# Gate tables copied after 70 row products instead of 76, one-hots of each half ahead of the GELU wait, and 14 instead of 16 row sums behind the first residual

## The chip, the cores and the metric

One core of a Trainium2 chip runs the whole program. The metric is device time in microseconds (us), the median over runs of the same program; smaller is better.

## What is computed

The program computes two transformer blocks over 256 tokens of width 1024, in float32. What matters here is the feed-forward part of the first block, which looks up single-neuron experts (8 heads, 16 experts of each head for every token, out of 16384):

```
def per_chunk(args):
    xc, ec, gc = args
    u = expert_u[ec]
    a = jnp.einsum('cd,chkd->chk', xc, u).astype(jnp.float32)
    w = (jax.nn.gelu(a) * gc).astype(xc.dtype)
    return jnp.einsum('chk,chkd->cd', w, expert_v[ec])
```

`ec` are the chosen experts of a token, `gc` their gates (a softmax over the chosen scores). The result is added to the residual stream, and the second block begins with matrix products on that sum.

## The kernel before

**Two ways to the same sum.** The 152 first tokens (DENSE) are computed densely: all 16384 experts, in 128 blocks of 128. An up block (L902, TensorE) is eight matmuls (16 records in the trace) into one PSUM bank; ScalarE takes its GELU (L1412) into the table `H`; VectorE multiplies `H` by the gates, which are zero for experts that a token didn't choose; a down block (L910) multiplies by the second weight table. The last 104 tokens are computed sparsely: for each of 107 pairs of columns a row of `u_rows` is fetched for each of 128 partitions (an indirect DMA issued by GpSimd, L2488, 128 rows of 4096 bytes), VectorE multiplies it by the token and adds up (L1901, a **row product**), the 107 results go through GELU and are weighed with their gates, and 107 fetched rows of `v_rows` are added up with these weights (L2022, a **row sum**; the first of each part is L2018).

**The fetches.** All 214 fetches go through seven buffers in one fixed order: products 0 to 95, sums 0 to 63, products 96 to 106, sums 64 to 106. GpSimd issues a fetch as soon as VectorE is through with the row seven places earlier. The two are called turns here: turn n is the n-th of these 214, and `row_turns(upto)` runs them until `upto` are done.

**The stream.** Weights come through a ring of four slots of 1 MB, loaded from the SyncE queue (L457). A slot holds two expert blocks and is loaded again when TensorE has used both.

**Order on TensorE.** The first 64 up blocks run with nothing between them. The gates and indices of the tokens (`routed`) are transposed ahead of the last eight of these (L942). Then TensorE waits for `sel_ready` (two copies of the transposed gate tables out of PSUM into `sel16`, VectorE, L2039) and goes into `mixed(0)`: up blocks 64 to 127, with `gates(0)` to `gates(18)` between them. Each is 16 small matmuls (L923) on one-hot tables of eight tokens, which VectorE writes in `one_hots` (L2055, L2056, L2058); they spread the gates over the experts of a half. `gates(0)` stands behind one block, `gates(1)` behind four more, and then three or four blocks lie between two of them. `gates(q)` waits for the one-hots q and for `apply_gates` q-2. `mixed(1)` is the same with down blocks 0 to 63 and `gates(19)` to `gates(37)` for the second half of the experts; 64 more down blocks follow.

**Order on VectorE.** 64 turns lie between the routing steps. `row_dots(DOTS_FIRST - dots_done[0])` brings them to 76, then come the two copies, and then the loop over the halves `hf` and the 19 groups `g`: the one-hots of g, `apply_gates` of g-1 (L2065, multiplies `H` in place, waits for TensorE's gates), and turns up to `a + (b - a) * (g + 1) // 19`, with (a, b) = (76, 116) in the first half and (116, 164) in the second. At the head of each half it waits until ScalarE's GELU has written that half of `H` (`expert_gelu`). Behind the loop come the remaining turns but the last 16 sums, the residual of the first 128 tokens (four times L2094, which TensorE's last down block releases), and the last 16 sums. TensorE meanwhile computes the first layer of the second block for tokens 0 to 127 (up to L1016), waits for all 107 sums, folds them in (L1029), and VectorE adds the residual of tokens 128 to 255.

Of the kernel before, what the change touches and what calls it, by code (L numbers as in the profile page):

```python
# [37 lines left out]
HALF_BLOCKS = EXPERT_BLOCKS // 2  # L38
# [14 lines left out]
DOTS_GATES = DOTS_EARLY + sum(DOTS_SCORES)  # L53
DOTS_SUMS = (4, 4, 4, 4, 3)
DOTS_PICK = 3
DOTS_FIRST = 76
TURNS_UP = 116
TURNS_DOWN = 164
GATES_AT = 22
WEIGH_AT = 8  # L60
WEIGH_GROUP = 7
LAST_ADDS = 16
ROWS = 7
U_FIRST = 96

# [90 lines left out]
class Count:  # L156
# [10 lines left out]
    def link(self, ins):  # L167

        self.inc(ins)
        self.eng.wait_ge(self.sem, self.n + self.more)  # L170


def build(nc, streams, small_d, first_d, second_d, mem_d, x_d, u_rows, v_rows, held_d, kv_scratch, out_d):
    ctx = ExitStack()
    with ctx:
# [3 lines left out]
        def sem(name):  # L179
            return ctx.enter_context(nc.semaphore(name))  # L180
# [214 lines left out]
        expert_psum, expert_gelu = sem("expert_psum"), sem("expert_gelu")  # L395
# [1192 lines left out]
        def _(dve):  # L1588
# [243 lines left out]
            for q in range(2):  # L1832
                dve.wait_ge(slot_done, START["merge"] + 2 * q + 2)
                for j in range(4):
                    n = 4 * q + j
                    tmp = merge_tmp.rearrange("p (b t) -> p b t", b=2)
                    g = gT.rearrange("p (b j) t -> p b j t", b=2)[:, :, n, :]
# [57 lines left out]
            def row_dots(count):  # L1895

                for m in range(dots_done[0], dots_done[0] + count):
                    f = u_fetch(m)
                    b = f % ROWS
                    dve.wait_ge(row_in[b], 16 * (f // ROWS + 1))  # L1900
                    dve.tensor_tensor_reduce(fetched[:, b, :], fetched[:, b, :], x_sparse[:, m // PAIRS_HALF, :], 1.0, 0.0, ALU.mult, ALU.add,  # L1901
                                             dots[:, 0, m:m + 1]).then_inc(dot_ready, 1)
                dots_done[0] += count
# [106 lines left out]
            def row_adds(count):  # L2010

                for m in range(adds_done[0], adds_done[0] + count):
                    f, part = v_fetch(m), m // PAIRS_HALF
                    b = f % ROWS
                    dve.wait_ge(row_in[b], 16 * (f // ROWS + 1))
                    total = sparse_sum[:, part, :]
                    if m % PAIRS_HALF == 0:
                        dve.tensor_scalar(total, fetched[:, b, :], dots[:, 0, m:m + 1], None, ALU.mult)\  # L2018
                            .then_inc(row_added, 1)
                    else:  # L2020
                        dve.wait_ge(row_added, m)
                        dve.scalar_tensor_tensor(total, fetched[:, b, :], dots[:, 0, m:m + 1], total,  # L2022
                                                 ALU.mult, ALU.add).then_inc(row_added, 1)
                adds_done[0] += count

            def row_turns(upto):

                for turn in range(dots_done[0] + adds_done[0], upto):
                    if turn < U_FIRST or U_FIRST + PAIRS_HALF <= turn < CHUNKS + PAIRS_HALF:
                        row_dots(1)  # L2030
                    else:
                        row_adds(1)

            row_dots(DOTS_FIRST - dots_done[0])

# [8 lines left out]
            def one_hots(g, q, b, hf, first=False):  # L2044

                if not first:
                    dve.wait_ge(gates_psum, q - 1)

                def key(j, n):
                    return sel16[:, j, g * GROUP:(g + 1) * GROUP].unsqueeze(2).to_broadcast([P, GROUP, n])  # L2050

                def numbers(a, n):
                    return iota16[:, a:a + n].unsqueeze(1).to_broadcast([P, GROUP, n])

                dve.tensor_tensor(e2[:, b], numbers(0, P), key(1, P), ALU.is_equal)  # L2055
                link(dve.tensor_tensor(e_same[:, b], numbers(hf * HEAD, HEAD), key(0, HEAD), ALU.is_equal))  # L2056
                gates_of = sel16[:, 2:4, g * GROUP:(g + 1) * GROUP].unsqueeze(3).to_broadcast([P, 2, GROUP, HEAD])
                dve.tensor_tensor(e1[:, b], e_same[:, b].unsqueeze(1).to_broadcast([P, 2, GROUP, HEAD]), gates_of,  # L2058
                                  ALU.mult).then_inc(e_ready, 1)

            def apply_gates(g, q, b, hf):

                dve.wait_ge(gates_psum, q + 1)
                h = H[:, hf * HALF_BLOCKS:(hf + 1) * HALF_BLOCKS, g * GROUP:(g + 1) * GROUP]
                dve.scalar_tensor_tensor(h, h, 1.0 / GSCALE, ps[:, 2 + b, :].rearrange("p (t n) -> p n t", t=GROUP),  # L2065
                                         ALU.mult, ALU.mult).then_inc(gates_applied, 1)

            def weigh(c, gelu, ready):

                dve.wait_ge(gelu, 1)  # L2070
                dve.tensor_tensor(dots[:, 0, c], dots[:, 1, c], pairs[:, 1, c], ALU.mult).then_inc(ready, 1)
                dve.wait_ge(ready, 1)

            for hf in range(2):
                dve.wait_ge(expert_gelu, HALF_BLOCKS * (hf + 1))
                for g in range(GROUPS):
                    if hf == 0 and g == WEIGH_GROUP:
                        dve.wait_ge(pairs_in, 16 * (3 + SETS_B))
                        weigh(slice(0, PAIRS_HALF), dot_gelu, weight_ready)
                    q = hf * GROUPS + g  # L2080
                    one_hots(g, q, q % 2, hf, first=(hf == 0 and g < 2))
                    if g:
                        apply_gates(g - 1, q - 1, (q - 1) % 2, hf)
                    a, b = ((DOTS_FIRST, TURNS_UP), (TURNS_UP, TURNS_DOWN))[hf]
                    row_turns(a + (b - a) * (g + 1) // GROUPS)
                apply_gates(GROUPS - 1, (hf + 1) * GROUPS - 1, ((hf + 1) * GROUPS - 1) % 2, hf)
            row_adds(PAIRS_HALF - adds_done[0])
            row_dots(CHUNKS - dots_done[0])
            weigh(slice(PAIRS_HALF, CHUNKS), dot_gelu_b, weight_b_ready)
            row_adds(CHUNKS - LAST_ADDS - adds_done[0])  # L2090

# [626 lines left out]
```

## Time and profile before

| | |
|---|---|
| median of 3 runs | 1790.42 us (1789.12 to 1792.3) |
| the profiled execution: time, span | 1789.55 us, 1787.8 us |
| granted TensorE clock, mean over the span | 0.992 |
| TensorE matmuls busy | 98% of the span |
| VectorE busy | 63% |
| ScalarE, GpSimd busy | 13%, 17% |

The profiled execution's time is 1.75 us more than its span. It lies 0.87 us below the median of the three runs. Times in the rows below are us from the span's start.

### The profile page before, as it was taken

The page shows a single profiled execution, that of the slowest core. Times are in us where ns is not written, and L with a number is a line of the kernel's source. Part 1 is how long each engine was busy: PE and PEld are TensorE (multiplying, and loading weights), DVE is VectorE, ACT ScalarE, POOL GpSimd, SP SyncE. Part 2 cuts the span into 40 slices and gives each one's busy share as a digit, 9 for nine tenths or more (in the row PEclk, how much of TensorE's full clock was granted, in tenths as well). Part 3 has the DMA queues.
Part 4 walks back from the last instruction along what each step waited for, and adds up shares of the span by engine and source line. Part 5 has one row for each costly group of instructions (what it writes and reads, how often), then busy time and mean ns, then how long its engine had stood idle before and what let it go on. Part 6 is the DMA issues. An engine that isn't in the chain of part 4 may idle for free.

```text
span 1787.8 us, 29568 instructions
## 1 busy us (share of the span) xinstructions
PE 1745.0 (98%) x11801; PEld 1491.0 (83%) x11801; DVE 1119.7 (63%) x2415; ACT 240.6 (13%) x599; POOL 296.9 (17%) x282
## 2 busy tenths in 40 slices
PE   8999999999999899999999999999999999999996
PEld 7888566986999899999999867799965988699942
DVE  4742432798666888799533453269974763379964
ACT  1014520111414111000000011111100001111100
POOL 0010000144333343344422200000000000000000
PEclk9999999999999899999999999999999999999998
DMA  7535234499999999999999953365444535354551
GB/s 273 189 118 165 71 118 142 158 332 374 414 417 416 376 381 390 346 415 415 415 417 417 350 223 118 121 250 172 166 165 165 169 138 171 123 178 166 168 179 54
DMA packets 76609, 439.62 MB, mean 246 GB/s; under 512 B 8578, under 2 KB 8656, under 8 KB 37840
## 3 DMA queue, kind: packets, MB, share of 16 engines
q1 hardware_dynamic: 42624, 305.15, 45.9%
q0 software_dynamic: 32592, 125.92, 18.2%
q10 hardware_dynamic: 1280, 6.95, 1.0%
q8 instruction: 82, 1.34, 0.3%
q14 instruction: 31, 0.25, 0.0%
HBM read 432.67 MB, written 5.24 MB: 245 GB/s over the span
## 4 chain that ended last, share of the span: by engine, by line
PE 80%; DVE 9%; DMA 9%; issue 1%; ACT 1%; POOL 0%; SPq 0%; DVEq 0%; POOLq 0%
PE ps L1128 16%; PE ps L910 14%; PE ps L529 10%; PE ps L902 8%; DMA arena<-u_rows,sparse_pairs 7%; PE ps L573 7%; PE ps L1166 4%; PE ps L612 3%; PE ps L487 3%; DVE arena L1901 2%; PE ps L765 2%; PE ps L812 2%; PE ps L778 1%; DVE arena L2022 1%; PE ps L923 1%
## 5 line engine op out<-in xcount | busy, mean ns | idle before, releaser
L902 PE MATMUL ps<-xT,ring 128*128 128x152 f32 x2048 | 271.9, 295 | 9.4 <-DVE sel L2039 9.4
L902 PEld LDWEIGHTS ps<-xT,ring 128*128 128x128 f32 x2048 | 267.6, 191 | 9.7 <-DVE sel L2039 9.6
L910 PE MATMUL ps<-arena,ring 128*128 128x152 f32 (+1 forms) x2048 | 269.6, 293 | 0.5 <-DMA ring<-stream 0.5
L910 PEld LDWEIGHTS ps<-arena,ring 128*128 128x128 f32 x2048 | 265.5, 190 | 1.2 <-issue 1.2
L529 PE MATMUL ps<-ring,arena 128*128 128x512 f32 x416 | 181.4, 592 | 0.4 <-ACT arena L1476 0.4
L2022 DVE SCALAR_TENSOR_TENSOR arena<-arena,sparse_dots 128x1024 f32<-128x1024 f32 x105 | 134.7, 1283 | 66.8 <-DMA arena<-v_rows,sparse_pairs 61.5
L1901 DVE CUSTOM_DVE_ANT_0 arena<-arena 128x1024 f32<-128x1024 f32 x107 | 128.1, 1223 | 71.1 <-DMA arena<-u_rows,sparse_pairs 70.6
L2488 POOL DMA_INDIRECT arena<-v_rows,sparse_pairs x107 | 132.7, 1241 | 233.3 <-DVE arena L2022 184.7
L2488 POOL DMA_INDIRECT arena<-u_rows,sparse_pairs x107 | 127.3, 1190 | 178.3 <-DVE sparse_dots L1901 154.4
L2451 POOL TENSOR_SCALAR stat<-stat 128x1 f32<-128x1 f32 (+2 forms) x23 | 4.4, 191 | 916.5 <-DVE stat L2192 705.1
L529 PEld LDWEIGHTS ps<-ring,arena 128*128 128x128 f32 x416 | 78.0, 190 | 93.0 <-issue 92.3
L573 PEld LDWEIGHTS ps<-xT,ring 128*128 128x128 f32 x1344 | 152.2, 192 | 3.0 <-issue 2.9
L573 PE MATMUL ps<-xT,ring 128*128 128x128 f32 x1344 | 153.2, 275 | 0.0
L1128 PE MATMUL ps<-arena 128*128 128x128 f32 x1128 | 133.6, 275 | 0.0
L1128 PEld LDWEIGHTS ps<-arena 128*128 128x128 f32 x1128 | 129.7, 192 | 0.0
L1128 PE MATMUL ps<-xT,ring 128*128 128x128 f32 x752 | 91.7, 275 | 0.0
L1128 PEld LDWEIGHTS ps<-xT,ring 128*128 128x128 f32 x752 | 87.7, 192 | 0.0
L487 PE MATMUL ps<-xT,ring 128*128 128x256 f32 x288 | 65.9, 391 | 0.0
L487 PEld LDWEIGHTS ps<-xT,ring 128*128 128x128 f32 x288 | 56.3, 197 | 8.0
L1412 ACT ACTIVATE arena<-ps 128x152 f32 x128 | 38.0, 297 | 181.5 <-PE ps L902 181.3
L1750 DVE CUSTOM_DVE_ANT_0 arena<-ps,small 128x128 f32<-128x128 f32 (+1 forms) x48 | 14.6, 354 | 76.1 <-PE ps L700 48.0
L1166 PE MATMUL ps<-arena 128*128 128x512 f32 x112 | 52.8, 594 | 0.3
(341 smaller groups left out, 2244.0 us busy)
## 6 DMA issues: line engine op xcount, KB each, us to landing
ring<-stream SPq DMA_DIRECT2D x288, 1024.0 KB, 7.4
arena<-second_params POOLq DMA_DIRECT2D x6, 1024.0 KB, 5.5
arena<-kv_scratch POOLq DMA_DIRECT2D x2, 2048.0 KB, 14.3
kv_scratch<-arena ACTq DMA_DIRECT2D x2, 1024.0 KB, 11.0
arena<-held_params ACTq DMA_DIRECT2D x1, 2048.0 KB, 16.6
arena<-u_rows,sparse_pairs POOLq DMA_INDIRECT x107, 14.3
arena<-v_rows,sparse_pairs POOLq DMA_INDIRECT x107, 14.4
arena<-second_params POOLq DMA_DIRECT2D x1, 1536.0 KB, 6.6
```

The source lines that it names most:

```text
L487: ins = pe.matmul(ps[:, bank, t * T:(t + 1) * T], w[:, k * 2 * P + t * P:k * 2 * P + (t + 1) * P], act[:, k, :], start=(k == 0), stop=(k = ...
L529: ins = pe.matmul(ps[:, bank0 + 2 * o + hf, :], act_of(2 * s + k, i), held[s][:, k * D + hf * 512:k * D + (hf + 1) * 512], start=(bank0 + ...
L573: ins = pe.matmul(ps[:, bank, t * T + i * P:t * T + (i + 1) * P], held[s][:, k * 2 * P + t * P:k * 2 * P + (t + 1) * P], xT[:, k, i * P:(i ...
L612: ins = pe.matmul(ps[:, b0 + b, half * T:(half + 1) * T], x[:, k, :], weight[:, k, :], start=(k == 0), stop=(k == 3))
L902: ins = pe.matmul(ps[:, o % 2, 0:DENSE], w[:, (o % 2) * D + k * P:(o % 2) * D + (k + 1) * P], xT[:, k, 0:DENSE], start=(k == 0), stop=(k = ...
L910: ins = pe.matmul(ps[:, 4 + k // 2, c:c + DENSE], w[:, (o % 2) * D + k * P:(o % 2) * D + (k + 1) * P], H[:, n, :], start=False, stop=last, ...
L1128: ins = pe.matmul(ps[:, bank + b, c * P:(c + 1) * P], weight[:, k, :], x[:, k, :], start=(k == 0), stop=(k == 3))
L1166: return pe.matmul(ps[:, bank, :], x, weight, start=(m == 0), stop=(m == FT_PAIRS - 1 and bank < 4))
L1412: act.activation(H[:, n, :], ps[:, b, 0:DENSE], ACT.Gelu_apprx_tanh).then_inc(expert_gelu, 1)
L1901: dve.tensor_tensor_reduce(fetched[:, b, :], fetched[:, b, :], x_sparse[:, m // PAIRS_HALF, :], 1.0, 0.0, ALU.mult, ALU.add, dots[:, 0, m: ...
L2022: dve.scalar_tensor_tensor(total, fetched[:, b, :], dots[:, 0, m:m + 1], total, ALU.mult, ALU.add).then_inc(row_added, 1)
L2488: pool.indirect_dma_start(fetched[:, b, :], None, table, bass.IndirectOffsetOnAxis(ap=pairs[:, 0, m:m + 1].bitcast(U32), axis=0), bounds_c ...
```

## The change

Three edits, all in VectorE's order:

1. The copies of the gate tables stand behind 70 turns instead of 76. The loop of the first half then starts at a = 74 (`DOTS_TURN`), so its first group runs turns up to 76 (six of them, where it ran two up to 78), and the later groups reach b = 116 as before.
2. The wait for `expert_gelu` moves from the head of a half to behind the one-hots of group 1, ahead of the first `apply_gates` of the half. The one-hots of groups 0 and 1, and the turns of group 0, no longer stand behind it, in both halves.
3. `LAST_ADDS` is 14 instead of 16: two row sums move from behind the first residual to ahead of it.

```diff
-DOTS_FIRST = 76
+DOTS_FIRST = 70
+DOTS_TURN = 74
...
-LAST_ADDS = 16
+LAST_ADDS = 14
...
             for hf in range(2):
-                dve.wait_ge(expert_gelu, HALF_BLOCKS * (hf + 1))
                 for g in range(GROUPS):
                     if hf == 0 and g == WEIGH_GROUP:
                         dve.wait_ge(pairs_in, 16 * (3 + SETS_B))
                         weigh(slice(0, PAIRS_HALF), dot_gelu, weight_ready)
                     q = hf * GROUPS + g
                     one_hots(g, q, q % 2, hf, first=(hf == 0 and g < 2))
+                    if g == 1:
+                        dve.wait_ge(expert_gelu, HALF_BLOCKS * (hf + 1))
                     if g:
                         apply_gates(g - 1, q - 1, (q - 1) % 2, hf)
-                    a, b = ((DOTS_FIRST, TURNS_UP), (TURNS_UP, TURNS_DOWN))[hf]
+                    a, b = ((DOTS_TURN, TURNS_UP), (TURNS_UP, TURNS_DOWN))[hf]
                     row_turns(a + (b - a) * (g + 1) // GROUPS)
```

## Rows read from the trace of the kernel before

**Rows 1.** The page, busy time, share of the span and instructions of each engine.
```profile
PE 1745.0 (98%) x11801; PEld 1491.0 (83%) x11801; DVE 1119.7 (63%) x2415; ACT 240.6 (13%) x599; POOL 296.9 (17%) x282
```
**Rows 2.** The page's groups: count, busy us, mean ns, idle before and its releaser.
```profile
L902 PE MATMUL ps<-xT,ring 128*128 128x152 f32 x2048 | 271.9, 295 | 9.4 <-DVE sel L2039 9.4
...
L910 PE MATMUL ps<-arena,ring 128*128 128x152 f32 (+1 forms) x2048 | 269.6, 293 | 0.5 <-DMA ring<-stream 0.5
```
**Rows 3.** Timeline of TensorE: start, duration, instruction, count, idle before.
```profile
559.66 1.04 PE L942 MATMUL ps<-small,arena 128*128 128x128 f32 x8
560.53 16.78 PE L902 MATMUL ps<-xT,ring 128*128 128x152 f32 x128
586.72 4.22 PE L902 MATMUL ps<-xT,ring 128*128 128x152 f32 x16 [9.40 <-DVE sel L2039]
590.78 0.63 PE L923 MATMUL ps<-e 128*128 128x64 f16 x16
591.24 8.51 PE L902 MATMUL ps<-xT,ring 128*128 128x152 f32 x64
599.59 0.63 PE L923 MATMUL ps<-e 128*128 128x64 f16 x16
...
722.60 0.63 PE L923 MATMUL ps<-e 128*128 128x64 f16 x16
```
**Rows 4.** Windows: length, then PE, PEld, DVE, ACT, POOL busy; clock; DMA share; GB/s.
```profile
577.40:580.40 3.00, 0.00 (x0) 0.00 (x0) 1.23 (x2) 0.30 (x1) 1.17 (x2) 0.99 0.99 408
...
586.70:590.70 4.00, 3.98 (x16) 3.98 (x17) 3.97 (x4) 0.00 (x0) 0.99 (x1) 0.51 1.03 409
```
**Rows 5.** Timeline of VectorE around the two copies, in the same columns.
```profile
566.75 1.23 DVE L1901 CUSTOM_DVE_ANT_0 arena<-arena 128x1024 f32<-128x1024 f32 x1 [1.90 <-DMA arena<-u_rows,sparse_pairs]
...
584.66 1.23 DVE L1901 CUSTOM_DVE_ANT_0 arena<-arena 128x1024 f32<-128x1024 f32 x1 [2.17 <-DMA arena<-u_rows,sparse_pairs]
...
585.81 0.85 DVE L2039 CAST sel<-ps 128x96 f16<-128x96 f32 x2
586.70 1.25 DVE L2055 TENSOR_TENSOR e<-iota,sel 128x1024 f16<-128x1024 f16 x1
587.87 0.68 DVE L2056 TENSOR_TENSOR e_same<-iota,sel 128x512 f16<-128x512 f16 x1
588.58 1.23 DVE L2058 TENSOR_TENSOR e<-e_same,sel 128x1024 f16<-128x1024 f16 x1
```
**Rows 6.** DMA queues in 545 to 580 us: stream (q1), row fetches (q0), MB moved.
```profile
q1 hardware_dynamic: 1186, 8.67, 59.9%
q0 software_dynamic: 1616, 5.86, 41.7%
```
**Rows 7.** The same in 740 to 865 us, inside the second mixed stage.
```profile
q1 hardware_dynamic: 3950, 28.82, 56.2%
q0 software_dynamic: 6070, 22.11, 44.3%
```
**Rows 8.** Both queues in 945 to 985 us.
```profile
q1 hardware_dynamic: 1515, 11.08, 66.9%
q0 software_dynamic: 1537, 5.61, 34.7%
```
**Rows 9.** Timeline of VectorE and TensorE where the second half begins.
```profile
732.04 1.23 DVE L2055 TENSOR_TENSOR e<-iota,sel 128x1024 f16<-128x1024 f16 x1 [8.09 <-ACT arena L1412]
...
736.91 0.28 PE L923 MATMUL ps<-e 128*128 128x64 f16 x4
```
**Rows 10.** Timeline of VectorE: the first residual and the last sums.
```profile
1010.80 1.42 DVE L2094 TENSOR_TENSOR xT<-ps,arena 128x256 f32<-128x256 f32 x4 [22.03 <-PE ps L910]
1012.14 22.11 DVE L2022 SCALAR_TENSOR_TENSOR arena<-arena,sparse_dots 128x1024 f32<-128x1024 f32 x16
```
**Rows 11.** Timeline of TensorE at the same place.
```profile
1025.46 7.03 PE L1016 MATMUL ps<-arena,xT 128*128 128x512 f32 x16
1034.30 3.77 PE L1029 MATMUL ps<-small,arena 128*128 128x64 f32 x32 [1.81 <-DVE arena L2022]
```

## The prediction

> **What bounds the kernel now.** I read the page first: TensorE's matmuls are busy for 98% of the span [rows 1], so a change on VectorE can only pay where TensorE waits for VectorE, or where it makes TensorE wait. The page's groups name the first such place: the up blocks stand idle for 9.4 us, all of it in front of the gate tables' copies, while the down blocks lose 0.5 us, to the stream [rows 2]. The timeline shows it as one stall: the last block ahead of the mixed stage ends at 560.53 + 16.78 = 577.31, the next begins at 586.72 [rows 3]. VectorE spends that time on row products that wait for their DMA; the copies come at 585.81, at once behind the twelfth of them [rows 5]. Their input has been there since the transposes of 559.66 [rows 3], so only VectorE's order holds them back. The second place is the end of the lookup: TensorE ends L1016 at 1032.49 and waits 1.81 us for the last sum [rows 11].
>
> **Edit 1, the copies after 70 turns.** The twelve products behind the routing steps become six. The sixth starts at 566.75 and ends 1.15 later (584.66 to 585.81 is one) [rows 5]; the copies take 0.85 and end at 568.8. That is 8.5 us before TensorE asks for them at 577.31. The stall of 9.40 us goes whole.
>
> **The clock behind the stall.** The granted clock is still 0.99 in the first 3 us of the idle time, and 0.51 while the first block after it runs [rows 4], that is 1.2 GHz and not 2.4. That block takes from 586.72 to 590.78, 4.06 us; four blocks at full clock take 591.24 to 599.59, 2.09 each [rows 3]. Without the stall nothing lowers the clock here, so 4.06 - 2.09 = 1.97 us come on top. The bounds are 0 (the clock falls all the same, in a short wait that takes the stall's place) and 1.97; I take 1.97, since TensorE was busy without a break up to 577.31.
>
> **What is late next.** The six moved products now stand between the one-hots 0 and 1. One-hots 0 start at 568.8 and take 588.58 + 1.15 - 586.70 = 3.03 [rows 5], so they are ready at 571.8, and `gates(0)`, behind one block at 579.4, doesn't wait. Then come turns 70 to 75 (counted from 0). Their rows land as before, because each fetch is released by the product seven places earlier and those for 70 to 75 are all released by products that don't move. The last of them is waited for at 584.66 [rows 5]. It ends at 585.81; one-hots 1 are ready 3.03 later, at 588.84. TensorE reaches `gates(1)` without a wait at 577.31 + 2.09 + 0.46 + 8.35 = 588.21 (block 64, the gates' 590.78 to 591.24, four blocks) [rows 3]. So a wait of 0.63 us takes the stall's place. Bounds: 0 if that row lands 0.6 us earlier, 3.8 if it lands one row's time later; at 3.8 the clock could fall again, and 2.0 more go. I take 0.63: up to 577 the two kernels ask the DMA for the same, and of what comes after, only the stream's reloads differ.
> `gates(1)` stood at 599.59 and comes to 588.84: 9.40 + 1.97 - 0.63 = 10.75 us (the last digit by rounding).
>
> **The rows afterwards.** In the stall the stream paused and the row fetches caught up; that rest is now gone, so I check whether VectorE can follow. A row fetch is 128 x 4096 B = 0.524 MB. Ahead of the mixed stage the row queue moves 5.86 MB in 35 us, 167 GB/s, a row every 3.13 us, beside a stream of 8.67 MB, 248 GB/s [rows 6]. In the second mixed stage, where gates stand between the blocks and the stream asks for less, it is 22.11 MB in 125 us, 177 GB/s, a row every 2.96 us, beside 231 GB/s of stream [rows 7]. What is needed: one-hots 18 stand behind turn 112, which is 37 rows behind the one of 584.66. With a row every p us, `gates(18)` can't come before 584.66 + 37p + 1.4 (a sum: 22.11 / 16) + 3.03. Without waits it comes 722.60 - 599.59 = 123.0 us after `gates(1)` [rows 3], at 711.9. The rows set the end only from p = (711.9 - 589.1) / 37 = 3.32. At 2.96 to 3.13 they cost nothing. The bound from the other side is the row queue of 945 to 985: 5.61 MB in 40 us, 140 GB/s, p = 3.74 [rows 8]. I take 2.96 to 3.13 because the stage differs from that of rows 7 only in up for down blocks.
> The GpSimd queue gets its releases for turns 77 and on up to 3.9 us later than in the kernel before (0.85 of copies and 3.03 of one-hots stand ahead of turn 70 now); the fetches are queued seven deep, and that is inside p. The stream's queue only follows TensorE.
> The wait for the GELU of the first half, now behind one-hots 1, is empty: ScalarE is through with block 63 soon after 577.31, VectorE comes there at 588.8.
>
> **Edit 2, second half.** VectorE waits 8.09 us for the GELU at 732.04 [rows 9]; it will fill this with one-hots 19, two sums and one-hots 20. TensorE gains nothing: `gates(19)` runs at 736.91, its one-hots were ready at 732.04 + 3.03 = 735.1 [rows 9]. Cost and gain are 0; VectorE's head start, 8 us at most, only helps to cover late rows. If that cover were gone, it would show as waits of `gates` in the second mixed stage. No instruction is added, and the fetches released earlier reach a queue in which the stream has its lead.
>
> **Edit 3, 14 sums.** Sixteen sums of 1.38 us end at 1034.25 [rows 10]; fourteen end 2.76 earlier, at 1031.5, before TensorE's own end of L1016 at 1032.49 [rows 11]. The wait of 1.81 goes whole, bounds 0 and 1.81. The two moved sums, and the release of their fetches, stand in VectorE's idle time of 22.03 us ahead of the first residual [rows 10]. With TensorE 10.75 us earlier, and two more sums at 3.74 us of a row, 22.03 - 10.75 - 7.5 = 3.8 us of it remain even if the rows don't come a microsecond sooner. What follows (residual of the second tokens, parameter load, normalization) hangs on L1029 and moves with it.
>
> **Sum.** 10.75 + 1.81 = 12.6 us. Against the profiled execution: 1789.55 - 12.6 = 1777.0. It was 0.87 below the median, so against the median 1790.42 - 12.6 = 1777.8.
>
> **Rivals.**
> A. *Rows a little too slow.* From p = 3.32 each 0.1 us costs 3.7: at 3.4 three us go, at 3.5 6.7, which leaves a gain of 5.9. Or the row for turn 75 lands one row's time late: 3.1 and the clock's 2.0 go, 7.5 remain. For it: nearly all of the DMA's time is taken, and rows of 3.74 exist. Against it: rows 6 and 7. It gives 1780.5 to 1785.
> B. *The other sign: rows at 3.74 through the first mixed stage.* Mechanism: the stream's queue is never empty, takes its full share, and VectorE's one-hots wait for rows group after group. `gates(18)` then comes at 584.66 + 37 x 3.74 + 4.4 = 727.4, 4.8 us later than before, less the 1.8 of edit 3: 3.0 slower, 1793.4. It decides from p = (722.6 + 1.8 - 589.1) / 37 = 3.66. For it: rows 8. Against it: there the stream took 277 GB/s of 417, more than TensorE's pace asks of it, as after a delay; in 545 to 580 it kept TensorE busy with 248 [rows 6, 8].
> The Trainium skill's page "DMA: Bandwidth & Descriptors", section "SWDGE vs HWDGE vs iDMA", says that a DMA engine takes its queues in turn. With rows in packets of 4096 B and the stream in packets of 8192 B, that rule would leave the rows a third of some 412 GB/s, an estimate of 3.8 us a row, and by it the sum would come out as rival B. The trace shows that third in 945 to 985; in 545 to 580 the rows had 167 of 415 GB/s.
> C. *Given back:* the sums come late before the first residual, and TensorE, which can't start the next block without it, gives the 10.75 back there. The slack of 3.8 us would have to be overrun by as much, three rows' time at 3.74. Only edit 3 stays: 1790.42 - 1.8 = 1788.6.
>
> **How the numbers follow.** Forecast 0.76, A 0.14, B 0.06, C 0.04. The forecast's own range is 1776 to 1780: at the low end no wait at `gates(1)` (0.6) and the scatter of the runs, some 1.5; at the high end 1.5 of small waits in front of gates and the scatter. For eight in ten I reach upward into A: 1775.5 to 1783.5. About 0.2% (3.6 us) is what a measurement of this kernel can tell from no change. Faster by more than that: forecast and A, 0.90; within: C, 0.04; slower: B, 0.06.
>
> **What would show it.** Copies (L2039) at 568; no idle time of TensorE named after them; the clock at 1.00 from 560 to 600; a wait of some 0.6 us in front of the second `gates`, then none; VectorE waiting for u rows in the first groups, where it didn't before; no wait for the last sums at L1029 (at about 1021), VectorE's idle time ahead of the first residual 4 to 15 us instead of 22. The prediction is wrong if TensorE stands in front of several `gates` of the first mixed stage, or if the clock falls again near 580 to 590.

## The result, and the profile after

The changed kernel takes 1774.93 us (median of 4 runs, 1774.62 to 1775.13), the kernel before 1789.77 in the runs beside it (1787.53 to 1792.3): ratio 0.991, 95% interval 0.9894 to 0.9927. That is 14.8 us faster, where the forecast was 12.6, and 0.6 us below the range of the forecast. The changed kernel's four runs lie within 0.5 us, those of the kernel before within 4.8. Two of the 66 runs of the kernel before in the experiments below took 2113 and 4723 us and are left out of every comparison.

The page's groups of the changed kernel, as [rows 2] (count, busy us, mean ns, idle before). Line numbers are one or two higher than before:

```profile
L911 PE MATMUL ps<-arena,ring 128*128 128x152 f32 (+1 forms) x2048 | 269.7, 293 | 0.4 <-DMA ring<-stream 0.4
L903 PE MATMUL ps<-xT,ring 128*128 128x152 f32 x2048 | 269.8, 293 | 0.0
```

The 9.4 us of idle time of the up blocks are gone, and they are busy 2.1 us less (269.8 for 271.9): the block at half clock. The timeline of TensorE at the place of [rows 3]:

```profile
558.00 1.04 PE L943 MATMUL ps<-small,arena 128*128 128x128 f32 x8
558.87 18.88 PE L903 MATMUL ps<-xT,ring 128*128 128x152 f32 x144
577.59 0.63 PE L924 MATMUL ps<-e 128*128 128x64 f16 x16
578.05 8.51 PE L903 MATMUL ps<-xT,ring 128*128 128x152 f32 x64
586.83 0.64 PE L924 MATMUL ps<-e 128*128 128x64 f16 x16 [0.26 <-DVE e L2059]
...
709.84 0.63 PE L924 MATMUL ps<-e 128*128 128x64 f16 x16
```

The block ahead of the copies and the one behind them are one piece now (144 records). `gates(1)` waits 0.26 us, and no later gates wait: from there to `gates(18)` it is 123.0 us, as before [rows 3]. Two windows (length, TensorE busy, granted clock, DMA share, GB/s) answer to [rows 4]:

```profile
577.30:586.70 9.40, 9.27 (x84) 1.00 1.01 410
586.70:591.00 4.30, 4.17 (x44) 1.00 1.05 428
```

On VectorE, as [rows 5]:

```profile
565.42 0.85 DVE L2040 CAST sel<-ps 128x96 f16<-128x96 f32 x2
566.31 1.25 DVE L2056 TENSOR_TENSOR e<-iota,sel 128x1024 f16<-128x1024 f16 x1
...
582.54 1.23 DVE L1902 CUSTOM_DVE_ANT_0 arena<-arena 128x1024 f32<-128x1024 f32 x1 [1.89 <-DMA arena<-u_rows,sparse_pairs]
...
583.69 1.22 DVE L2056 TENSOR_TENSOR e<-iota,sel 128x1024 f16<-128x1024 f16 x1
```

The copies end 9.4 us before TensorE reaches the wait for them (566.27 and 558.87 + 16.78 = 575.65); the products that they were queued behind now end at 583.69, and one-hots 1 follow at once.

The end of the lookup, as [rows 10, 11]: 14 sums in 19.33 us, and L1030 starts where L1017 ends.

```profile
997.95 1.42 DVE L2096 TENSOR_TENSOR xT<-ps,arena 128x256 f32<-128x256 f32 x4 [22.23 <-PE ps L911]
999.28 19.33 DVE L2023 SCALAR_TENSOR_TENSOR arena<-arena,sparse_dots 128x1024 f32<-128x1024 f32 x14
```
```profile
1012.61 7.03 PE L1017 MATMUL ps<-arena,xT 128*128 128x512 f32 x16
1019.47 3.66 PE L1030 MATMUL ps<-small,arena 128*128 128x64 f32 x32
```

**Where the profiled pair differs.** The span fell by 15.0 us, 1787.8 to 1772.8. Of these 1.66 arose long before the change: the transposes stand at 558.00 instead of 559.66. There the clock was at 1.2 GHz for a shorter time near 90 us. Windows of the kernel before and of the changed kernel, same columns:

```profile
80.00:100.00 20.00, 20.00 (x94) 0.83 0.28 105
```
```profile
80.00:100.00 20.00, 20.00 (x102) 0.91 0.31 109
```

The code there is the same. In fourteen profiles of this study the mean clock of that window was 0.83 three times, 0.91 twice and 1.00 nine times, whatever the kernel (the changed one shows 0.91 and, profiled again, 0.83): chance of an execution. What is left is 11.10 at `gates(1)` (599.59 - 1.66 - 586.83), 1.81 in front of L1029, and 0.4 more. Of this, 0.3 lies at L1029 too: from the start of L1016 to that of L997 behind L1029 it is 12.44 us before and 10.35 after, 2.09 less, of which 1.81 is the wait. So the profiled pair confirms the two terms of the sum, 10.75 and 1.81, and does not explain why the medians differ by 2.3 us more. The experiments do.

### The profile page after: what moved, and what is told of

Read it like the earlier page. It is cut to its first block, busy times and chain, and to the rows that moved or that the text cites. A ratio compares the mean times of both kernels' runs of the same rounds, so it can differ in the third digit from the quotient of the medians.

```text
span 1772.8 us, 29569 instructions
## 1 busy us (share of the span) xinstructions
PE 1741.4 (98%) x11801; PEld 1488.1 (84%) x11801; DVE 1119.1 (63%) x2415; ACT 240.9 (14%) x599; POOL 301.4 (17%) x282
## 4 chain that ended last, share of the span: by engine, by line
PE 81%; DMA 9%; DVE 8%; issue 1%; ACT 1%; POOL 0%; SPq 0%; POOLq 0%; DVEq 0%
PE ps L1129 16%; PE ps L911 14%; PE ps L530 10%; DMA arena<-u_rows,sparse_pairs 7%; PE ps L574 7%; PE ps L903 7%; PE ps L1167 4%; PE ps L613 3%; PE ps L488 3%; DVE arena L1902 2%; PE ps L766 2%; PE ps L813 2%; PE ps L779 1%; PE ps L924 1%; PE ps L998 1%
## 5 line engine op out<-in xcount | busy, mean ns | idle before, releaser
L903 PE MATMUL ps<-xT,ring 128*128 128x152 f32 x2048 | 269.8, 293 | 0.0
## 6 DMA issues: line engine op xcount, KB each, us to landing
arena<-v_rows,sparse_pairs POOLq DMA_INDIRECT x107, 12.6
```

Source lines behind the costliest of these rows:

```text
L903: ins = pe.matmul(ps[:, o % 2, 0:DENSE], w[:, (o % 2) * D + k * P:(o % 2) * D + (k + 1) * P], xT[:, k, 0:DENSE], start=(k == 0), stop=(k = ...
```

## Experiments

All are compared with runs of the kernel before on the same chip, in three groups (experiments 1 to 4; 5 to 8; 9 to 12); ratios are to it. Its median was 1789.5, 1791.4 and 1791.5 us in the three groups. "X us faster" is worked out from the ratio and its 95% interval; differences between the medians of two runs are called so.

**1. The kernel before, once more** (no edit).

> The kernel before, unchanged, profiled once more and timed against itself. Two theories of the 2.3 us that the change gained beyond the forecast of 12.6. M, chance of one profile: in the profiled execution before, the granted clock stood at 1.2 GHz for 6.8 us behind the narrow matmuls of 86 us, in the one after for 3.4 us, which moves everything behind it by 1.66 us; the code there is the same, so another profile of the same kernel should show either length. N, a real cost of the stall: each execution of the kernel before pays for its clock behind the stall of 9.4 us, and differently each time. Both expect a ratio of 1.000 and a scatter of 2 us or more; M expects the early stretch to be sometimes 3.4 us; N expects the half-clock stretch behind the stall (10.24 us) to differ between executions. A third theory, that the change has a further effect, expects both stretches as before.

Measured: 1793.15 us, ratio 1.0013 (1.0001 to 1.0024), from 1788.6 to 1795.3. This is the same kernel, and yet the interval leaves out 1: a difference of 0.1% between two kernels is not evidence here. The early stretch is absent in this profile, so its length is chance (M). But the span is 2.8 us longer than in the first profile, and the larger part of the reason is a place that none of my theories named. Timeline of TensorE behind the last sums, and a window over it:

```profile
1032.23 6.04 PE L1029 MATMUL ps<-small,arena 128*128 128x64 f32 x32 [1.80 <-DVE arena L2022]
1038.07 10.02 PE L997 MATMUL ps<-xT,ring 128*128 128x128 f32 x64
```
```profile
1034.00:1046.00 12.00, 12.00 (x68) 0.60 0.46 174
```

The wait is the same 1.8 us as in [rows 11], but behind it the granted clock fell to 1.2 GHz for most of 12 us. L1029 takes 6.04 us instead of 3.77, L997 10.02 instead of the 7.39 that the first profile shows: 4.9 us, in an execution of the same program. Behind the stall at the copies the block takes 4.42 us and the gates 1.06, where [rows 3] has 4.22 and 0.63. So N holds too: that stall's clock cost differs between executions. Counted from the start of the block behind the stall to `gates(1)`, less the 10.90 us (2.09 + 0.46 + 8.35) that this work takes at full clock, it is:

| profile | stall, us | clock behind it, us |
|---|---|---|
| before, first | 9.40 | 1.97 |
| before, again | 9.92 | 2.81 |
| edit 2 alone | 9.56 | 1.51 |
| edit 3 alone | 9.33 | 3.02 |
| 15 sums | 9.40 | 1.70 |
| wait at L1029 filled | 9.39 | 2.76 |

The mean is 2.3 us; the 1.97 of the profile read first lies in the middle.

**2. Edit 1 alone.**

```diff
-DOTS_FIRST = 76
+DOTS_FIRST = 70
+DOTS_TURN = 74
...
-                    a, b = ((DOTS_FIRST, TURNS_UP), (TURNS_UP, TURNS_DOWN))[hf]
+                    a, b = ((DOTS_TURN, TURNS_UP), (TURNS_UP, TURNS_DOWN))[hf]
```

> Only edit 1: copies behind 70 turns, the wait for the GELU stays at the head of each half. Theory: copies at 568, VectorE then waits for the GELU of the first half until about 577.8; one-hots 0 are ready at 580.8 and TensorE waits 1.4 us in front of gates(0), then about 1.1 in front of gates(1) (six products end at 587.7, one-hots 1 at 590.8). gates(1) at 590.8 instead of 599.6: 8.8 us faster than before, about 1781; both waits are too short for the clock to fall. Rival: edit 2 adds nothing to edit 1, because the wait for the GELU is over when VectorE comes; then 10.8 to 13 us faster, 1777 to 1779.

Measured: 1782.56 us, ratio 0.9959 (0.9944 to 0.9974), 7.3 us faster (4.7 to 10.0), where 8.8 was expected. TensorE and VectorE:

```profile
577.69 0.64 PE L924 MATMUL ps<-e 128*128 128x64 f16 x16 [1.61 <-DVE e L2059]
578.17 8.51 PE L903 MATMUL ps<-xT,ring 128*128 128x152 f32 x64
587.56 0.64 PE L924 MATMUL ps<-e 128*128 128x64 f16 x16 [0.88 <-DVE e L2059]
```
```profile
574.55 1.22 DVE L2056 TENSOR_TENSOR e<-iota,sel 128x1024 f16<-128x1024 f16 x1 [9.16 <-ACT arena L1413]
```

VectorE has the tables and then waits 9.16 us for the GELU, and two waits of 1.61 and 0.88 us take the stall's place, 2.5 us against 0.26 with edit 2 (0.26 to 1.45 in the four profiles that have edits 1 and 2 as changed). So edit 1 moves the critical wait onto the GELU, and edit 2 is what takes it away from there. Behind the last sums, where this kernel still has 16, the clock fell too (L1030 took 5.64 us, L998 8.80).

**3. Edit 3 alone.**

```diff
-LAST_ADDS = 16
+LAST_ADDS = 14
```

> Only edit 3: 14 sums behind the first residual. Theory: TensorE's wait of 1.81 us in front of L1029 is gone and nothing else moves: 1.8 us faster. Rival: the edit gains up to 2.8 us (two sums of 1.38), since more than TensorE's wait hangs on VectorE there. Second rival: nothing, since the residual of the second tokens or the parameter load sets the time.

Measured: 1785.26 us, ratio 0.9971 (0.9959 to 0.9983): 5.2 us faster (3.0 to 7.3). All three expectations miss: 1.8, 2.8 and 0. In its profile L1029 follows L1016 without a gap and takes 3.66 us. The gain is 3.4 us more than the wait; it has the size of the clock's cost in experiment 1.

**4. The clock kept up over the stall.**

```diff
+FILL = 9
...
             up_turn(HALF_BLOCKS // 8 - 1, 8, 0, HALF_BLOCKS // 8 - 1)
+            pe.wait_ge(zeros_ready, 1)
+            pe.wait_ge(xkv_ready, 16)
+            for _ in range(FILL):
+                pe.matmul(ps[:, 6, :], zeros[:], zeros[:].unsqueeze(1).to_broadcast([P, 4, P]),
+                          start=True, stop=True)
             pe.wait_ge(sel_ready, 2)
```

> The kernel before with nine matmuls of zeros (128 x 512, into PSUM bank 6, which nothing reads) between the last block ahead of the mixed stage and the wait for the gate tables. They compute nothing that is used. The stall stays, its clock cost goes: each takes 0.86 us, so TensorE is busy for 7.7 of the 9.4 us. Theory of the prediction: the block behind the stall takes 2.09 us and not 4.06, 2.0 us faster than before, about 1787.8. Theory N (the stall's clock cost is larger and varies): 2.5 us or more faster, and less scatter than the kernel before has. Rival: no gain, because the clock falls all the same in the last 1.7 us of idle time or behind them.

Measured: 1790.22 us, ratio 0.9996 (0.9985 to 1.0008), by time no difference, though the interval reaches to 2.7 us faster, so by time the forecast 2.0 isn't excluded either. The trace says what happened:

```profile
573.97 7.89 PE L949 MATMUL ps<-zeros 128*128 128x512 f32 x18
584.19 2.33 PE L903 MATMUL ps<-xT,ring 128*128 128x152 f32 x16 [2.33 <-DVE sel L2045]
587.33 0.64 PE L924 MATMUL ps<-e 128*128 128x64 f16 x16 [0.81 <-DVE e L2064]
```

The block runs at full clock (2.33 as a piece, before 4.22 [rows 3]), but it is now shorter than one-hots 0, which start with it, and 0.81 us of the gain are waited away at `gates(0)`. So the block does get its full clock back, and part of that gain can't be had alone. The 2.33 us of waiting behind the zeros were not followed by a fall of the clock (1.00 over 577.3 to 600).

**5. Edits 1 and 2 without edit 3** (the changed kernel with `LAST_ADDS = 16`).

> Edits 1 and 2 without edit 3: 16 sums behind the first residual. Theory K (the wait in front of L1029 costs its 1.8 us and, in most executions, a fall of the granted clock behind it, which in the three profiles that show it took 3.3 to 4.9 us): the time is 4 to 6 us above that of the changed kernel (1774.9), 1779 to 1781, and scatters by 3 us or more. Rival S (edit 3 is worth its 1.8 us, the rest of the surplus comes from edits 1 and 2): 1776.7, with a scatter of 0.5 us.

Measured: 1779.55 us, ratio 0.994 (0.9926 to 0.9954), 4.6 us above the changed kernel's first median (1774.93) and 3.2 above the one of experiment 10 (1776.36, on another chip). Its six runs spread over 3.0 us. The first difference and the spread are as theory K has them, the second difference is smaller than its 4 to 6 us; rival S (1776.7) lies 1.7 us below the fastest of the six runs, and even counted from experiment 10 (1778.2) it lies below all of them. Its L1030 took 5.50 us and its L998 8.94, behind a wait of 1.81.

**6. 15 sums instead of 16, in the kernel before** (`LAST_ADDS = 15`).

> The kernel before with 15 sums instead of 16 behind the first residual. TensorE's wait in front of L1029 shrinks from 1.81 to 0.43 us. If the clock falls only behind the longer wait, this gives nearly all of edit 3 (measured alone: 0.9971): 1.4 of waiting and the 3 to 5 of the clock, ratio 0.997. If any wait there lets the clock fall, only the 1.4 us: ratio 0.9992, and the profile may show 1.2 GHz behind it. Rival S: 1.4 us, no clock.

Measured: 1784.78 us, ratio 0.9969 (0.9958 to 0.998), the same as with 14 sums alone. The wait shrank to 0.41 us and the clock stayed:

```profile
1029.47 3.77 PE L1029 MATMUL ps<-small,arena 128*128 128x64 f32 x32 [0.41 <-DVE arena L2022]
1033.06 7.39 PE L997 MATMUL ps<-xT,ring 128*128 128x128 f32 x64
```

1.4 us less of waiting gained 5.6. One of the two moved sums was enough.

**7. The wait in front of L1029 filled, in the kernel before.**

```diff
+FILL = 7
...
             ab_u(0)
+            for _ in range(FILL):
+                pe.matmul(ps[:, 0, P:2 * P], zeros[:], zeros[:], start=True, stop=True)
             pe.wait_ge(row_added, CHUNKS)
```

> The kernel before with seven matmuls of zeros (128 x 128, into columns of PSUM bank 0 that the next product overwrites) ahead of the wait for the last sum. They compute nothing that is used, and take some 1.5 of the 1.81 us that TensorE waits there. The sums end when they did, so L1029 starts when it did. Theory K: the clock stays at 2.4 GHz behind it, 2 to 4 us faster than before in the median (ratio about 0.998), less scatter. Rival S: no difference. Second rival: the clock falls all the same, since it is the low activity of the 64-column matmuls behind the wait that lets it fall, not the wait.

Measured: 1789.11 us, ratio 0.9991 (0.9981 to 1.0001), 1.6 us faster with an interval that just reaches no change, so by time, with the 0.1% that experiment 1 shows between equal kernels, neither theory K nor rival S is excluded. The profile has the clock at full speed behind it:

```profile
1029.80 1.73 PE L1027 MATMUL ps<-zeros 128*128 128x128 f32 x14
1031.78 3.77 PE L1032 MATMUL ps<-small,arena 128*128 128x64 f32 x32 [0.25 <-DVE arena L2025]
1035.37 7.39 PE L998 MATMUL ps<-xT,ring 128*128 128x128 f32 x64
```

The narrow matmuls of L1032 alone don't bring the clock down, then. But the median lies 4.3 us above that of experiment 6, on the same chip, and only some 1.4 us of that are the later start of L1032. The mean granted clock of its twelve runs goes down to 0.991, where the nine of experiment 6 have 0.993 to 0.995 and the kernel before has 0.990 to 0.994. So the clock was low for longer in some of its executions than in any of experiment 6. Whether that was behind the filled wait, behind the stall or near 90 us isn't shown; this stays open.

**8 and 9. One row less ahead of one-hots 1** (the changed kernel with `DOTS_TURN = 73`), in two groups, the second beside the changed kernel.

> The changed kernel with 73 instead of 74 as the start of the first half's turns: the first group runs turns up to 75 instead of 76, so one-hots 1 come one row earlier (some 3 us). Theory: the wait of 0.26 us in front of gates(1) goes and nothing takes its place, 0.3 us faster than the changed kernel, 1774.6, which is at the edge of what can be measured; profile without a wait of TensorE for the one-hots. Rival: the later groups then carry one row more (43 in 18 steps), and a wait of 0.3 us or more appears further on: same or slower.

> The same as turn73, beside the changed kernel on one chip. turn73 showed no wait for one-hots at all. Theory: 0.3 us faster than the changed kernel, which five rounds can hardly tell. Rival: 2 us faster, as the medians of two different chips had it (1772.9 against 1774.9); then something else than that wait is involved.

Measured: 1772.85 us, ratio 0.9908 (0.9893 to 0.9922), and 1774.3 us, ratio 0.9909 (0.9889 to 0.9929). No wait of TensorE for one-hots is left. Against the changed kernel in experiment 10 it is 2 us faster in the median, with runs of 1772.6 to 1776.0 against 1773.7 to 1777.1. The fastest and the slowest run are both 1.1 us faster. The wait that is gone was not always 0.26 us: the four profiles with the same code up to `gates(1)` show 0.26, 0.73, 1.45 and 0.77 us (first, experiments 10, 5 and 12), 0.8 in the mean. From the transposes to `gates(1)` it is 28.4 us in both profiles with 73, and 29.4 in the mean of those four. So about 1 us is what the traces explain, and nothing else need be involved; by time alone the two kernels can't be told apart with so few runs.

**10. The changed kernel once more** (no edit).

> The changed kernel once more, to be set beside the next kernel on the same chip and to show its stretches of 1.2 GHz a second time. Theory K: no stretch between the mixed stage and the end of the lookup, since no wait of 1.8 us is left there; the only ones are the early one near 89 us, which may be absent, and the one at the end of the program. Ratio 0.991.

Measured: 1776.36 us, ratio 0.9917 (0.99 to 0.9934). Its profile has 1.2 GHz near 90 us (0.83 over 80 to 100) and at the program's end only.

**11. Edit 2 alone.**

> Only edit 2: the one-hots of groups 0 and 1 ahead of the wait for the GELU, copies still behind 76 turns and 16 sums at the end. Theory: no difference, ratio 1.000, in the first half because the GELU is over long before the copies, in the second because TensorE doesn't wait for one-hots there; VectorE's 8 us of waiting at 732 shrink to some 5 in front of the gates. Rival: the rows run ahead in the second half and the stream is held up, or the ends of the sums move: slower or faster by 1 us or more.

Measured: 1789.63 us, ratio 0.9997 (0.9985 to 1.001), no difference, as expected. VectorE in the second half:

```profile
727.79 1.23 DVE L2058 TENSOR_TENSOR e<-e_same,sel 128x1024 f16<-128x1024 f16 x1
734.13 0.69 DVE L2065 SCALAR_TENSOR_TENSOR arena<-arena,ps 128x512 f32<-128x512 f32 x1 [5.12 <-PE ps L923]
```

The 8.09 us of [rows 9] have become 5.12, and TensorE, which doesn't wait for VectorE there, gains nothing. Here, too, the clock fell behind the wait of 1.80 us at L1029 (0.73 over 1034 to 1046).

**12. Eight more turns in the first mixed stage** (the changed kernel with `TURNS_UP = 124`).

> The changed kernel with 124 instead of 116 turns in the first mixed stage: one-hots 18 stand behind turn 120 and not 112, so 45 rows instead of 37 must land in the same 123 us, one every 2.73. This tests the bound of the prediction, that rows set the end of the stage once they need less than the 2.96 us that they take. Theory: TensorE waits for one-hots in several groups; with rows at 2.96 gates(18) comes at the landing of the row of turn 75 + 45 x 2.96 + 4.4, some 10 us later than in the changed kernel, 1784 to 1786. Rival: the seven buffered rows and a faster row queue cover it, and the time stays at 1775.

Measured: 1779.88 us, ratio 0.9941 (0.992 to 0.9962), 3.5 us above the median of the changed kernel beside it (four and five runs). TensorE waits in three of the nineteen gates:

```profile
585.74 0.64 PE L924 MATMUL ps<-e 128*128 128x64 f16 x16 [0.77 <-DVE e L2059]
...
594.55 0.64 PE L924 MATMUL ps<-e 128*128 128x64 f16 x16 [1.88 <-DVE e L2059]
...
677.60 0.71 PE L924 MATMUL ps<-e 128*128 128x64 f16 x16 [2.43 <-DVE e L2059]
678.12 8.06 PE L903 MATMUL ps<-xT,ring 128*128 128x152 f32 x48
...
715.08 0.63 PE L924 MATMUL ps<-e 128*128 128x64 f16 x16
```

Behind the longest of them the three blocks take 8.06 us instead of 6.45: the clock again (0.79 over 678.0 to 686.2). The row of turn 75 was used at

```profile
581.45 1.23 DVE L1902 CUSTOM_DVE_ANT_0 arena<-arena 128x1024 f32<-128x1024 f32 x1 [2.14 <-DMA arena<-u_rows,sparse_pairs]
```

`gates(18)` comes 129.3 us after `gates(1)` and not 123.0: 4.3 us of waits and some 1.7 of the clock. The mechanism (rows set the pace once they must come faster than they do) holds. The size was forecast too large, some 10 us, where `gates(18)` came 6.3 later and the median rose by 3.5; the rows came faster than 2.96 us: with 4.4 behind the last, (715.08 - 581.45 - 4.4) / 45 = 2.87 at most.

## Why the prediction was right, and where it was wrong

**Right.** The stall of 9.40 us goes whole, its clock cost of 1.97 with it, and a wait in front of `gates(1)` takes its place, 0.26 us where 0.63 was forecast (its row came sooner). 11.10 measured in the profiled pair, 10.75 forecast. Over all profiles the three sizes are 9.5, 2.3 (1.5 to 3.0) and 0.8 (0.26 to 1.45), 11.0 together; that the one profile read for the forecast lay near these means is luck, the mechanism is not. The rows keep up: from 600 to 718 us they moved 20.68 MB, p = 2.99. VectorE waited for rows at the head of the stage, and TensorE for none beyond the 0.26 us at `gates(1)`. Of rivals A and B nothing showed; experiment 12 shows that the bound exists and where a wait then appears. Edit 2 costs and gains nothing by itself (experiment 11), and edit 1 without it leaves 2.5 us of waiting (experiment 2), which the forecast's reading of the GELU wait implied and didn't say.

One reading was wrong and touches no term: "In the stall the stream paused". In 577 to 587 us the stream moved 2.00 MB (200 GB/s) beside 2.09 MB of rows. It paused behind the stall: 1.19 MB in 587 to 600 (92 GB/s), and there the rows had 3.08 MB (237 GB/s).

**Wrong: the price of the wait in front of L1029.** The step was "The wait of 1.81 goes whole, bounds 0 and 1.81". Its wall time is right (1.81 us gone). The term left out is the clock. The profile that I read happened to show no fall there; five of the six profiles with 1.8 us of waiting there do, and none of the eight with 0.41 us or less (line numbers of the kernel before):

| kernel | wait | L1029 / L997, us | clock over 1015 to 1050 |
|---|---|---|---|
| before, first profile | 1.81 | 3.77 / 7.39 | 1.00 |
| before, again | 1.80 | 6.04 / 10.02 | 0.85 |
| edit 1 alone | 1.80 | 5.64 / 8.80 | 0.90 |
| clock kept over the stall | 1.81 | 4.65 / 9.79 | 0.90 |
| edits 1 and 2 | 1.81 | 5.50 / 8.94 | 0.90 |
| edit 2 alone | 1.80 | 4.41 / 10.03 | 0.90 |
| 15 sums | 0.41 | 3.77 / 7.39 | 1.00 |
| wait filled | 0.25 | 3.77 / 7.39 | 1.00 |
| edit 3 alone | none | 3.66 / 7.39 | 1.00 |
| the changed kernel twice, experiments 8, 9, 12 | none | 3.66 / 7.39 | 1.00 |

The price where it fell is 3.3 us four times and 4.9 once; over the six 3.0 in the mean. The sum with it is 10.75 + 1.81 + 3.0 = 15.6, for 14.8 measured, and edit 3 alone comes to 4.8, for 5.2 measured. The prediction prices the clock behind the long wait and puts it at nothing behind the short one, without giving a reason; the one profile behind it shows 1.00 there. The bound from the other side should have come from this kernel's own row for a block at half clock: with L1029 and L997 wholly at half clock (3.77 + 7.39 us) it would be some 11 us more, and the range would have reached below 1775.5.

**Wrong, without effect on the time: the slack of the rows.** I forecast 4 to 15 us of idle time of VectorE ahead of the first residual; it is 22.23 (22.03 before [rows 10]). I had let the rows keep their absolute times. In fact their fetches are released by VectorE, which in the mixed stages follows TensorE, so they moved with it: in the first mixed stage the DMA queues now carry 411 GB/s where a like window before had 386. The idle time is as good as before, and rival C had nothing to stand on.

**Chance.** 1.66 us of the profiled pair's difference come from the clock near 90 us, which varies between executions of one program (0, 1.6 or 3.3 us). With the clock behind the stall (1.5 to 3.0) and behind the wait at L1029 (0 to 4.9) it has the size of the scatter of the kernel before, over 7 us (1787.07 to 1794.81 in the first group).

## What to carry to other kernels

A wait's price on TensorE is its length and what the clock takes behind it, and the second part can be the larger one and can be missing from the one execution that was profiled: profile the kernel before twice, or look at the scatter of its runs, before a wait of a microsecond or two is priced at its length. Where an engine does work that nobody is waiting for ahead of work that somebody is, move the second up, and then look for the next wait in that engine's queue: here the copies alone ran into the GELU wait (experiment 2). A stream of transfers that an engine releases itself moves with that engine; don't hold it fixed when the engine gets faster.

## What the runs showed of the hardware

- A wait of 1.8 us on TensorE was followed by a fall to 1.2 GHz in five of six profiles, and waits of 0.41 and 0.25 us at the same place were not (one profile each). A wait of 2.43 us in the middle of dense work (experiment 12) was followed by one; waits of 1.88, 1.61 and 1.45 us in such a place (experiments 12, 2 and 5), and of 2.33 us behind matmuls of zeros (experiment 4), were not. So the length of the wait alone doesn't decide; what else does isn't shown.
- The same stall of 9.3 to 9.9 us cost 1.5 to 3.0 us more through the clock behind it, in six profiles.
- Near 86 to 90 us, in or behind 32 matmuls of 24 columns, the clock fell in five of fourteen profiles with no wait at all, at a cost of 1.6 or 3.3 us (the transposes of L659 start at 124.14 us where the window's clock is 1.00, at 125.75 where it is 0.91, at 127.42 where it is 0.83).
- In 945 to 985 us row fetches and weight stream moved nearly the same number of packets, 1537 and 1515, of 3.7 and 7.3 KB in the mean, and so shared the DMA one to two: 140 and 277 GB/s [rows 8]. Where the stream took 231 to 248 GB/s, the rows had 167 to 177 [rows 6, 7], and a row came every 2.87 us or less in experiment 12.
